# Low parts of eight weight units formed by GpSimd instead of DVE, in the second layer of a two-layer encoder

## The reference

```
kvs = rmsnorm(x, kv_norm_g) @ w_kv_shared          # keys and values for layer 1
shared_k1, shared_k2 = rotary_partial(kd...)       # the first 16 columns of each head are rotated
q1, q2 = rotary_partial(qd...)                     # qd from h @ w_q_b
a = masked_softmax(s1, mask) - lam * masked_softmax(s2, mask)
o = rmsnorm(a @ v, subln_g) * (1.0 - lam_init)
x = x + concatenate([o, y_mem]) @ w_out[1]
x = x + moe_swiglu(rmsnorm(x, ffn_norm_g[1]), ...)
```

## Time and profile before

| what | value |
|---|---|
| median of 3 runs | 1451.46 us (1451.25 to 1451.56) |
| the profiled execution: time | 1451.6 us |
| the profiled execution: span of the core | 1449.9 us |
| mean granted clock of TensorE | 0.996 of 2.4 GHz |
| busy: PE, DVE, ACT, GpSimd | 1421.1, 1151.6, 951.0, 41.6 us |
| low parts by DVE (L1057), whole kernel | 397 listed in the page's group, 905.7 us |

### The profile page before, as it was taken

How to read it: one execution, slowest core, us unless ns; L and a number is a source line. 1 busy time by engine, 2 the same in 40 slices (tenths; PEclk the granted TensorE clock), 3 DMA queues, 4 the chain that set the end, 5 groups by cost and what they waited for, 6 DMA issues and landing times.

```text
span 1449.9 us, 20488 instructions
## 1 busy us (share of the span) xinstructions
PE 1421.1 (98%) x7668; PEld 1206.3 (83%) x7668; DVE 1151.6 (79%) x1021; ACT 951.0 (66%) x873; POOL 41.6 (3%) x71
## 2 busy tenths in 40 slices
PE   7999999999998999999999999999999999999997
PEld 6997999998887788888888888888888888888885
DVE  6675555456776898898889888888888898988997
ACT  5545433435456677777777777777777777777775
POOL 2000000000001000000000000000000000001100
PEclk9999999999999999999999999999999999999999
DMA  9643455554532999999999999999999999999992
GB/s 303 213 132 132 148 186 185 197 196 161 175 117 106 344 375 378 385 377 370 384 377 382 384 368 384 379 376 374 386 370 383 378 377 376 375 388 365 323 372 112
DMA packets 207067, 438.38 MB, mean 302 GB/s; under 512 B 7216, under 2 KB 54320, under 8 KB 207008
## 3 DMA queue, kind: packets, MB, share of 16 engines
q1 hardware_dynamic: 202880, 423.65, 80.7%
q0 software_dynamic: 4128, 13.93, 2.7%
HBM read 431.79 MB, written 5.77 MB: 302 GB/s over the span
## 4 chain that ended last, share of the span: by engine, by line
PE 93%; DVE 3%; ACT 2%; issue 1%; DMA 0%; DVEq 0%; ACTq 0%; POOLq 0%
PE bank L1781 29%; PE bank L1783 29%; PE bank L1782 29%; PE bank L2373 2%; DVE wlo L1057 1%; ACT whi L667 1%; PE bank L1902 0%; PE bank L2285 0%; PE bank L1940 0%; PE bank L2215 0%; PE bank L1921 0%; PE bank L1966 0%; PE bank L1907 0%; DMA gain<-in_mem_norm_g_dram 0%; PE bank L1796 0%
## 5 line engine op out<-in xcount | busy, mean ns | idle before, releaser
L1057 DVE TENSOR_TENSOR wlo<-raw,whi 128x2048 fp32r<-128x2048 f32 x397 | 905.7, 2289 | 180.8 <-ACT whi L667 179.4
L667 ACT CAST whi<-raw 128x2048 fp32r<-128x2048 f32 x397 | 758.1, 1914 | 211.2 <-PE bank L1783 211.0
L1781 PE MATMUL bank<-whi,op_hi 128*128 128x512 f32 (+1 forms) x1176 | 442.6, 376 | 4.6 <-DVE op_lo L1410 2.1
L1783 PE MATMUL bank<-whi,op_lo 128*128 128x512 f32 (+1 forms) x1176 | 434.7, 370 | 0.0
L1782 PE MATMUL bank<-wlo,op_hi 128*128 128x512 f32 (+1 forms) x1176 | 434.2, 369 | 0.0
L1781 PEld LDWEIGHTS bank<-whi,op_hi 128*128 128x128 f32 x1176 | 221.7, 189 | 46.7 <-DVE wlo L1057 5.2
L1783 PEld LDWEIGHTS bank<-whi,op_lo 128*128 128x128 f32 x1176 | 221.6, 188 | 38.2
L1782 PEld LDWEIGHTS bank<-wlo,op_hi 128*128 128x128 f32 x1176 | 221.8, 189 | 35.3
L1781 PE MATMUL bank<-whi,h2T_hi 128*128 128x512 f32 x544 | 214.4, 394 | 0.9 <-DVE h2T_lo L1454 0.5
L1783 PE MATMUL bank<-whi,h2T_lo 128*128 128x512 f32 x544 | 212.6, 391 | 0.0
L1782 PE MATMUL bank<-wlo,h2T_hi 128*128 128x512 f32 x544 | 212.6, 391 | 0.0
(11 more groups left out here) (308 smaller groups left out, 787.3 us busy)
## 6 DMA issues: line engine op xcount, KB each, us to landing
raw<-in_w_gate_up_moe_dram SPq DMA_DIRECT2D x223, 1024.0 KB, 7.2
raw<-in_w_down_moe_dram SPq DMA_DIRECT2D x109, 1024.0 KB, 7.3
raw<-in_w_gate_up_dense_dram SPq DMA_DIRECT2D x22, 1024.0 KB, 5.3
raw<-in_w_down_dense_dram SPq DMA_DIRECT2D x11, 1024.0 KB, 5.1
raw<-in_w_in_a_dram SPq DMA_DIRECT2D x10, 1024.0 KB, 13.6
raw<-in_w_out_dram SPq DMA_DIRECT2D x8, 1024.0 KB, 5.0
raw<-in_w_kv_shared_dram SPq DMA_DIRECT2D x6, 1024.0 KB, 5.4
raw<-in_w_mem_kv_dram SPq DMA_DIRECT2D x4, 1024.0 KB, 6.3
```

Of the source, the lines that this page charges most:

```text
L667: a.copy(whi[:, c % SPLIT, :], src).then_inc(hi_ready, 1)
L1057: d.tensor_tensor(wlo[:, c % SPLIT, :], src, whi[:, c % SPLIT, :].bitcast(F32), ALU.subtract).then_inc(lo_ready, 1)
L1781: m.matmul(dst, sh, mh, start=start and i == 0, stop=False)
L1783: last = m.matmul(dst, sl, mh, start=False, stop=stop and i == n - 1)
```

## The change

The low parts of units 24 to 31 are formed by GpSimd. The two places in DVE's turns that formed them are taken out. GpSimd waits until the low part of unit 23 is there, then for each high part in turn, and subtracts as DVE did. ACT's `head_squares` waits for its own previous squares from the second head on, since all write the same scratch tile. DVE waits for all of GpSimd's low parts before it forms the first low part of the experts.

```diff
@@ gpsimd @@
             load_gain(6, 22)
+            pool.wait_ge(lo_ready, U_KV + 6)
+            for p in range(24, P_END):
+                c = unit_of(p)
+                pool.wait_ge(hi_ready, c + 1)
+                g.tensor_tensor(wlo[:, c % SPLIT, :], raw[:, ring(c) % RAW, :], whi[:, c % SPLIT, :].bitcast(F32),
+                                ALU.subtract).then_inc(lo_ready, 1)
             pool.wait_ge(gain_in, 16 * 3)
@@ scalar @@
             def head_squares(h):
                 act.wait_ge(o_out, h + 1)
+                if h:
+                    act.wait_ge(o_squared, h)
@@ vector @@
                 if i == 7:
                     head_norm(0)
-                if i == 0:
-                    split_lo(U_KV + 6)
-                if c == 1 and i < 9:
-                    split_lo(unit_of(p) + 3)
                 if i:
                     applied_dve(i - 1)
@@
             head_pair_lo(2)
+            dve.wait_ge(lo_ready, U_MOE)
             split_lo(U_MOE)
```

## The result

The changed kernel takes 1462.64 us (median of 4 runs, 1462.04 to 1464.88). The kernel before, on the same chip, takes 1451.51 us (1451.25 to 1452.77). The ratio is 1.0075, with a 95% interval of 1.0063 to 1.0087: 11.1 us slower. The profiled execution took 1462.04 us with a span of 1460.3 us, 10.4 us more than the span before.

A forecast was written before the change was run, and what follows sets the result against it. PE was taken to bound the kernel (busy 98% of the span), so DVE edits count only where PE stands still. Terms 5.2 + 1.7 + 2.7 + 2.7 + 0.3 = +12.6 us gave 1464.1 us; range 1449.3 to 1467.0.

The forecast's parts named there:

- the two bounds: For a two-input DVE instruction during GpSimd's subtraction: it pays nothing, or the rest of GpSimd's 4.8 us; the second was taken.
- the opposite 0.22: The chance given to DVE never waiting for GpSimd, which leaves only the gain: -1.7 us, 1449.8 us.
- turn 0, up to the transposes of probabilities, with its clock fall: Low parts 24 and 25 hold unit 22's rotation; transposes L1986 come 5.2 us later, plus 1.7 us for a lowered clock.
- rotation of unit 25 under low part 28: GpSimd holds this rotation until it ends at 422.3; PE's transposes move from 419.66 to 422.4: +2.7 us.
- rotation of unit 26 under low part 29: GpSimd runs until 430.0, this rotation until 431.0; its transposes, at 428.38 before, come later: +2.7 us.
- The first clock fall: After PE's 6.9 us stand near 390, the clock falls as it did after the earlier 2.7 us wait: +1.7 us.
- The last 0.3 us: Low part 31 on GpSimd until 451.7 makes DVE's L1354, at 451.39, start later: +0.3 us at most.
- Rival 1: Unit 22's last two rotation instructions pass together at the first seam; +5.9 to +7.8, 1457.4 to 1459.3 us; chance 0.25.
- Rival 2: DVE never waits for GpSimd, so only the gain is left: -1.7 us, 1449.8 us; chance 0.22.
- Rival 3: GpSimd takes over 8.2 us a unit; PE waits for low part 24; within the rest's 0.07, shared with DVE slowed.
- Rival 4: The clock falls also after both 2.7 us stands: up to 2 x 1.7 more, 1467.5 us; forecast's upper part, together 0.46.
- the gain of 1.7 us: PE's wait before transposes L1986 at 395.65 goes, since DVE's maxima start without 4.49 us of low parts ahead.

The follow-up runs named there:

- e1_halves: The changed kernel with each GpSimd subtraction cut into two instructions of 1024 elements a partition; 1460.03 us.
- e6_units28_29_only: The kernel before with only the low parts of units 28 and 29 on GpSimd, the other six on DVE; 1457.98 us.
- e7_quarters: The changed kernel with each GpSimd subtraction cut into four instructions of 512 elements a partition; 1457.78 us.
- e10_other_four: The kernel before with only the low parts of units 26, 27, 30 and 31 on GpSimd, the other four on DVE; 1453.11 us.
- e5_unit24_only: The kernel before with only unit 24's low part on GpSimd, the other seven on DVE; 1452.43 us.
- e8_four_waits: The changed kernel, GpSimd waiting for the rotations ahead of units 24, 25, 28, 29, and for turn 4's scaled probabilities ahead of unit 26; 1450.59 us.
- e3_dve_reordered: The kernel before, nothing on GpSimd, with DVE forming low part 25 in turn 2 instead of turn 0; 1449.75 us.
- e2_rot_first: The changed kernel, GpSimd waiting until DVE has finished the rotations that low parts 24, 25, 28 and 29 would cut into; 1455.41 us.

## Why the prediction was right

It forecast 1464.1 us; 1462.64 was measured. The step that decided it was the choice between the two bounds, a held instruction or none. No row of the kernel before showed DVE held; the prediction took it from the reverse case and gave the opposite 0.22, so this was a well-founded bet and not a reading. Its mechanism, that GpSimd's instruction keeps DVE out to its end just as DVE's keeps GpSimd out, is what the rows show, and halving and quartering the piece halved and quartered the price. That is also what the Trainium skill says in "SBUF — State Buffer", section "Who interferes with whom" (whoever issues first has the shared pair for its whole instruction), and the runs agree by 4.46, 2.30 and 1.20 us.

Term by term, each measured where the prediction placed it, less a start that is 0.16 us earlier:

| term | forecast | measured |
|---|---|---|
| turn 0, up to the transposes of probabilities, with its clock fall | 5.2 + 1.7 | 5.5 (401.03 - 395.65 + 0.16) |
| rotation of unit 25 under low part 28 | 2.7 | 2.3 |
| rotation of unit 26 under low part 29 | 2.7 | 2.4 |
| the rest of the stage | 0.3 | 0.3 |
| sum | 12.6 | 10.5 |

- *GpSimd's duration* was put at 4.8 us, from twice a product of half the columns. It was 4.55 to 4.61, and 9.04 for the first two together. That is 0.2 us or more for each, so it makes most of the 0.4 and 0.3 us by which the second and third terms were too large. In the first term, the two of them and the steps between make 0.9 of the 1.4 us: the stand was to end at 397.4 and ended at 396.32, of which 0.16 is the earlier start. The Trainium skill's page "GPSIMD Engine Reference" ("Performance versus the Vector engine") has 4497 ns for a tensor_tensor of this size, which lies within 3% of the trace.
- *The first clock fall* was put at 1.7 us, like the one of the earlier trace rows. The prediction took it to begin when PE goes on. It begins while PE stands (0.63 in 392 to 394, 0.50 in 394 to 396), so part of it fell on no work. The work between the two transposes, put at 3.5 us at full speed, took 401.03 - 396.32 = 4.7: the fall cost 1.2 us there.
- *The last 0.3 us* had the right size but named the wrong instruction. L1354 was not what low part 31 caught; the tensor_scalar L1357 in front of it was (0.82 us, up to 461.59; GpSimd until 461.57). The transposes of heads ahead of it lie 10.10 us later than in the kernel before (449.92 against 439.82), those behind it 10.34 (464.59 against 454.25).
- *Nothing for the waits and for units 26, 27 and 30* held: 1451.38 us for the waits, no new stand for those units.
- *Rival 1* (both sums through together at the first seam) is out: two DVE instructions, one at each seam, with whole units, halves and quarters. *Rival 2* (DVE never waits) is out by the rows of after. *Rival 3* is out: PE never waited for a low part. *Rival 4* did not happen in this profiled execution (the run of 1464.88 us had the lowest mean clock, 0.992 against 0.993 or 0.994; no trace shows whether it happened there). But it is no separate case: with the same stands the clock fell twice in e1_halves, e6_units28_29_only and e7_quarters. What decides it is open. No run was made for it alone; a stand's length alone doesn't, since the clock fell behind 1.7 us in e10_other_four and not behind 2.7 us in e5_unit24_only.

Where the gain of 1.7 us went is shown from two sides. The maxima were freed from 4.49 us of subtractions and at once put behind 8.9 us of held sums; in e8_four_waits and e3_dve_reordered, where nothing holds the sums, the gain is there.

## What to carry to other kernels

Before moving an elementwise step from DVE to an idle GpSimd, list what DVE and PE do during GpSimd's longer instruction, not how idle GpSimd is: every DVE instruction there with two SBUF inputs (and, as shown below, a tensor_scalar too) costs what is left of that instruction, and it counts in full if PE waits for it. Two long GpSimd instructions back to back are far worse than one, since DVE gets one instruction through at each seam. If the aim is only that a step leaves a busy spot on DVE, first try a later place for it on DVE: that gave the same gain here, and putting two engines' steps behind the critical one together gave 4.6 us.

## What the runs showed of the hardware that was not expected

- A tiny DVE instruction with one tensor input in SBUF is held too. The tensor_scalar on 128x2 elements (L1357) took 1.39 and 0.82 us in the changed kernel, and 2.79 us in e2_rot_first (L1359 there), ending with GpSimd's instruction; one on 128x256 took 2.47 us rather than 0.35 in e1_halves (L1373). The reciprocal just before it was not held (0.18 us, at 449.44, inside low part 30), nor were the maxima, which read PSUM (L1345 at 407.38, inside low part 26, took 0.41 us). The Trainium skill has this in the same section of "SBUF — State Buffer", which counts tensor_scalar among the instructions that can take the shared pair; the trace agrees. The sum of the prediction took only instructions with two SBUF inputs, and so missed it; only its rival 1 allowed for one.
- A held instruction looks like a slow one: on the page DVE's busy share stays at 79% with 18.2 us of work less. Only the duration of single rows gives it away.
- The clock fell to 0.50 while PE did nothing, so here a part of the fall cost nothing: 1.2 us of work were lost behind the stand of 5.84 us, and 1.6 behind the one of 2.67 us in the kernel before.
- The clock fall behind a stand of 1.7 to 2.8 us comes in some executions of a kernel and not in others: e2_rot_first's eleven runs spread from 1451.19 to 1456.85 us, with the mean clocks given above.
